# Moving a seven-product block form from six gate chunks to nine other projection chunks, on one Trainium2 core

## The chip, the cores and the metric

The kernel runs on one core of a Trainium2 chip. TensorE (PE) multiplies, VectorE (DVE), ScalarE (ACT) and GpSimd (POOL) do the rest, SyncE (SP) issues nearly all loads. The metric is the device time of one execution in microseconds, lower is better. All arithmetic that matters here is in float32; each float32 matmul stands in the trace as two records.

## The reference, cut to what matters

256 tokens of width 1024 pass through two layers:

```
# first block
proj = norm(x) @ w_in            # heads of three attention branches A, B, M, their z, and 3072 gate logits
o_a, o_b, o_m = attention(...)   # sparse, latent and memory attention, 512 wide each
branch_n = (o_n * silu(z_n)) @ w_branch[n]
x = x + sum_n(sigmoid(gates_n) * branch_n) @ w_out
# second block
x = x + mixer(norm(x))           # dq, dk, dv: differential attention; gq, gk, gv, gg, gr: gated linear attention; w_o
x = x + cross_attention(norm(x), norm(mem_2))   # keys and values: mem_2 @ w_ckv, 1024 x 2048
x = x + mixture_of_experts(norm(x))             # 32 experts of 3 matrices, 201 MB of weights in all
```

## The kernel before, in words

**Chunks and slots.** The projection weights come in chunks of mostly 1024 x 512 (2 MB), listed in `chunks` (lines 300 to 344) in the order of use: mk, mv, cq, small, qi, uq, ukv, qa, ka, va, za, zb, qm, zm, then gate00, gate01, wb0, gate10, gate11, wb1, gate20, gate21, wb2, then wout0, wout1, ckv0, gr, gqk, dq, dk, gv, ckv1, gg, dv, ckv2, wo0, wo1, ckv3, wcq0, wcq1, wco0, wco1. Chunk c goes to slot c % 4 of `ring`; SP waits, chunk by chunk in this order, until the job that read the chunk four before it has ended (line 1134). After them come the experts' weights, 96 loads of 2 MB into ten buffers (lines 1156 to 1190); those of the first round are held back by `wcq`, by attention C and by x3, later ones by the expert job that read the buffer before.

**Projections on TensorE.** `project` (line 488) keeps 128 tokens x 128 inputs of x stationary and streams 512 columns of weights: 16 matmuls for a chunk, the result by tokens. `project_t` (line 513) keeps weights stationary and streams the 256 tokens: 32 matmuls for a chunk, the result transposed. Both write one of two PSUM banks `ACC` of 1024 columns, taken in turn; a job waits until the bank's user two jobs before has been drained. `spread` and the `after` arguments put attention steps (`attend`: scores S, transposes T, outputs O) between the matmuls of a chunk. VectorE masks and normalizes the scores, ScalarE takes the exponentials and copies the transposes.

**The block form** (`project_blocks`, line 624) is used for the six gate chunks. Weights and x are each cut into 2 x 2 blocks; seven products of blocks replace eight, as in Strassen's scheme in Winograd's form. The weight block is stationary, in tiles of 128, and 128 tokens stream: 7 x 8 = 56 matmuls of 128 columns. A job takes two `ACC` banks, "low" for four products and "high" for three. The sums of blocks of x (`T_x`) and of weights (`S_a`, `S_b`, and two made in place) are POOL's (lines 1291 to 1318): of each gate chunk four additions of 1024 columns, each followed by a wait for itself; the first may start when the chunk before has had its fourth product, the last after this chunk's fourth. VectorE's `gate_blocks` (line 1931) combines the products in eight operations of 256 columns, which read PSUM; ScalarE then takes the tanh from SBUF.

**The order around it.** TensorE: zb with attention A; qm; zm with attention B; gate00 and gate01 with attention M; wb0; gate10, gate11, wb1; gate20, gate21, wb2; transposes of mem_2; wout0, wout1; ckv0, in which x1 is transposed; gr, gqk, gate_z; dq, dk, gv, ckv1; transposes of dq and dk; the GLA products ("intra", "kend"); gg; states; dv; ckv2 and ckv3 with attention DA; wo, wcq, attention C, wco, router, experts. VectorE's order (line 1923 on): heads of A, A, heads of qm, B, M, merging of the three branches (line 1967), `drain_rows` of mem_2, a reciprocal root (`rsqrt`, line 1658, 12 small steps each waiting for the one before), x updated from wout0 and wout1 (`add_to_x`), the norm of x1 (line 2002), the decay chain of the gated attention (lines 2009 to 2019, with eight scans), the padding products (line 2027, six operations, each of two SBUF inputs), heads of dq and dk (line 2030). ScalarE drains qm, dq, dk, gv and the ckv chunks from PSUM with copies. Between decay steps (`decay_a`, `decay_e`) ScalarE takes exponentials (lines 1547 to 1550); on `decay_e` POOL makes the three products QP, QN, KE (line 1333), which TensorE needs for "intra".

A line that sets the pace of the loads, and the two that take a bank:

```
1134  wait_full(sp, last_job[chunks[c - RING][0]])
472   if n >= 2:
473       pe.wait_ge(acc_free[n % 2], n // 2)
```

Of the kernel before, what the change touches and what calls it, by code (L numbers as in the profile page):

```python
# [20 lines left out]
ALU = mybir.AluOpType  # L21
# [3 lines left out]
P = 128  # L25
D = 1024
S = 256
# [18 lines left out]
RING = 4  # L46
# [10 lines left out]
def two_block_layer(nc, A, out):  # L57
    ctx = ExitStack()
    with ctx:
# [128 lines left out]
        gate_chunks = [f"gate{n}{h}" for n in range(3) for h in range(2)]  # L188
        T_x = R2[:, :].rearrange("p (i k q) -> p i k q", i=4, k=4)
        S_a, S_b = (R5[:, 2048 + 1024 * i:3072 + 1024 * i].rearrange("p (k n) -> p k n", k=4) for i in range(2))  # L190
# [44 lines left out]
        x_sums = sem("x_sums")  # L235
        w_sums = sem("w_sums")
        block_products = sem("block_products")
        gate_sums = sem("gate_sums")
        gate_tanh = sem("gate_tanh")
# [97 lines left out]
        ckv_chunk(2)  # L337
        for h in range(2):
            chunks.append((f"wo{h}", 512, [(0, cols(A["w_o_2"][0], h * 512, h * 512 + 512))]))
        ckv_chunk(3)  # L340
# [5 lines left out]
        landed_value, seen = [], [0] * RING  # L346
        for c, (_, _, parts) in enumerate(chunks):
            seen[c % RING] += 16 * len(parts)
            landed_value.append(seen[c % RING])

        def slot_of(name):
            c = chunk_at[name]
            width = chunks[c][1]
            k = SLOT // width
            return slots[c % RING][:, 0:k * width].rearrange("p (k n) -> p k n", k=k)
# [3 lines left out]
        acc_no, aux_no, aux_uses, last_job = {}, {}, [0] * 4, {}  # L359
# [70 lines left out]
        for t in range(TT):  # L430
# [20 lines left out]
        stream = [slots[4], slots[5]] + [slots[chunk_at[name] % RING] for name in ("wcq0", "wcq1")] + spare[0:2] + [  # L451
            slots[chunk_at[name] % RING] for name in ("wco0", "wco1")] + spare[2:4]
# [15 lines left out]
        def _(pe):  # L468
            def acc(key):
                n = len(acc_no)  # L470
# [150 lines left out]
            def x_block(i, j):  # L621
                return XT3[:, 4 * i:4 * i + 4, j * P:(j + 1) * P]

            def project_blocks(name, after=None):

                c = gate_chunks.index(name)
                wait_chunk(name)
                w = slot_of(name)

                def w_block(i, j):  # L630
                    return w[:, 4 * j:4 * j + 4, 256 * i:256 * i + 256]

                if c == 0:
                    pe.wait_ge(x_sums, 4)
                low, low_full = acc((name, "low"))
                products = [(w_block(0, 0), x_block(0, 0), None, False), (w_block(0, 1), x_block(1, 0), None, True),
                            (S_a, T_x[:, 0], 1, False), (S_b, T_x[:, 1], 3, True),
                            (w_block(1, 0), T_x[:, 2], 3, False), (w_block(1, 1), T_x[:, 3], None, True),
                            (S_b, x_block(1, 1), 4, False)]
                for m, (left, right, sums, last) in enumerate(products):  # L640
# [3 lines left out]
                    if sums:  # L644
                        pe.wait_ge(w_sums, 4 * c + sums)
                    for j in range(2):
                        for k in range(4):
                            mm = nc.tensor.matmul(bank[:, j * P:(j + 1) * P], left[:, k, j * P:(j + 1) * P], right[:, k, :],  # L648
                                                  start=(k == 0), stop=(k == 3))
                            if m == 6 and (j, k) == (1, 3):  # L650
                                mm.then_inc(high_full, 1)
                            elif last and (j, k) == (1, 3):
# [3 lines left out]
                            if after:  # L656
                                after(m * 8 + j * 4 + k + 1)
                last_job[name] = (name, "high")
# [95 lines left out]
            project("qm", XT3)  # L754
# [8 lines left out]
            def start_m(done):  # L763
# [5 lines left out]
                if done == 14:  # L769
# [4 lines left out]
                if done in (14, 22, 30, 38):  # L774
                    attend("M", (done - 14) // 8, (done - 14) // 8 + 1)

            def end_m(done):
                if done in (6, 18, 30):
                    attend("M", 4 + (done - 6) // 12, 5 + (done - 6) // 12)

            project_blocks("gate00", start_m)
            project_blocks("gate01", end_m)
# [3 lines left out]
            for n in (1, 2):  # L786
                project_blocks(f"gate{n}0")
                project_blocks(f"gate{n}1")
# [8 lines left out]
            def merged_half(i):  # L797
                if i % 4 == 0:
                    pe.wait_ge(merged_ready, i // 4 + 1)

            R1T = kt(R1[:, :], KD)
            project("wout0", R1T, ready=merged_half)
            project("wout1", R1T)

            wait_turned("mem2")
            project("ckv0", R2T, after=lambda done, total: turn_rows("x1", 1) if done == total - 3 else None)
# [9 lines left out]
            project("dq", XT3)  # L816
            project("dk", XT3)
            project("gv", XT3)
            project("ckv1", R2T)
# [21 lines left out]
            project("gg", XT3)  # L841
# [284 lines left out]
        def _(sp):  # L1126
# [5 lines left out]
            for c, (name, width, parts) in enumerate(chunks):  # L1132
                if c >= RING:
                    wait_full(sp, last_job[chunks[c - RING][0]])
                for first, src in parts:
# [5 lines left out]
                    sp.dma_start(dst, src).then_inc(slot_landed[c % RING], 16)  # L1141
# [5 lines left out]
                if name == "wout0":  # L1147
                    wait_full(sp, ("gate21", "high"))
# [62 lines left out]
        def _(pool):  # L1211
# [83 lines left out]
            for t in range(TT):  # L1295
                for h in range(2):
                    wait_full(pool, ("kb", t, h))
            xb = [[XT3[:, 4 * i:4 * i + 4, j * P:(j + 1) * P] for j in range(2)] for i in range(2)]
            add(T_x[:, 0], xb[0][1], xb[0][0], ALU.subtract, x_sums, 1)
            add(T_x[:, 1], xb[1][1], T_x[:, 0], ALU.subtract, x_sums, 2)  # L1300
            add(T_x[:, 2], xb[1][1], xb[0][1], ALU.subtract, x_sums, 3)
            add(T_x[:, 3], T_x[:, 1], xb[1][0], ALU.subtract, x_sums, 4)
            for k in range(2):
                wait_full(pool, ("S", first_unit["B"] + len(units["B"]) - 1 - k))
            for c, name in enumerate(gate_chunks):
                pool.wait_ge(slot_landed[chunk_at[name] % RING], landed_value[chunk_at[name]])
# [965 lines left out]
```

## Time and profile before

| | |
|---|---|
| median of 3 runs | 1144.57 us (1144.38 to 1144.93) |
| the profiled execution | 1144.48 us, span 1142.8 us |
| granted TensorE clock, mean | 0.925 |
| busy: TensorE, VectorE, ScalarE, POOL | 83%, 30%, 15%, 9% |
| HBM traffic | 290 MB |

A profile is read from the whole to the part: which stretch is bound by what (the table of stretches), what an instruction takes start to start in a dense stretch (the timeline of one engine), and which wait ended last. In rows of the timeline the first number is the start in us, the second the length of the group, in brackets the idle time before it and what ended it. BIG, R, PJ and SQE are names of buffers in SBUF, buffer numbers left out.

### The profile page before, as it was taken

What the parts mean: (1) busy time and instruction counts of PE and PEld (TensorE: products, weight loads), DVE (VectorE), ACT (ScalarE), POOL (GpSimd) and SP (SyncE); (2) the same over time, 40 slices, a digit from 0 to 9 for tenths busy, and PEclk for the clock granted to TensorE, in tenths of its full rate; (3) what the DMA queues carried; (4) which work ended last, traced back from release to release, by engine and by line L of the source; (5) the groups of instructions that cost most, each with busy time, mean ns of one, the idle gap of its engine ahead of it and who ended that gap; (6) DMA issues with size and microseconds to landing.
All of it is one profiled execution on the core that took longest, in us unless ns stands there. A gap on an engine that the chain in (4) does not pass through costs nothing.

```text
span 1142.8 us, 11530 instructions
## 1 busy us (share of the span) xinstructions
PE 944.0 (83%) x4742; PEld 532.3 (47%) x4742; DVE 341.3 (30%) x879; ACT 175.3 (15%) x380; POOL 102.6 (9%) x121
## 2 busy tenths in 40 slices
PE   7999999899999999999999999665655556474737
PEld 3555485679999465455544554221221213131312
DVE  3217934764232221525644523100010101010101
ACT  2114232441000012212311312000000000000000
POOL 2013110135343010100000000000000000000000
PEclk9999999999999999999999999888777869787879
DMA  9546232224444264432208548999999999999996
GB/s 328 175 157 218 83 142 74 74 74 145 151 148 180 81 220 147 147 125 96 74 1 316 205 191 356 428 428 428 427 428 428 427 428 428 427 427 428 428 421 271
DMA packets 64308, 290.33 MB, mean 254 GB/s; under 512 B 9015, under 2 KB 11902, under 8 KB 52222
## 3 DMA queue, kind: packets, MB, share of 16 engines
q1 hardware_dynamic: 63966, 289.04, 63.9%
q8 instruction: 39, 0.64, 0.2%
q10 hardware_dynamic: 288, 0.52, 0.1%
q14 instruction: 15, 0.12, 0.0%
HBM read 288.51 MB, written 1.05 MB: 253 GB/s over the span
## 4 chain that ended last, share of the span: by engine, by line
PE 63%; DMA 28%; DVE 5%; ACT 2%; issue 1%; SPq 0%; DVEq 0%; ACTq 0%
PE ACC L505 24%; PE ACC L520 8%; PE AUX L1038 6%; PE ACC L648 6%; DMA ring<-in_w_e_up_dram 5%; PE ACC L544 4%; PE AUX L1074 4%; DMA BIG<-in_w_e_up_dram 3%; DMA ring<-in_w_e_down_dram 3%; DMA PJ<-in_w_e_up_dram 3%; DMA PJ<-in_w_e_gate_dram 3%; DMA BIG<-in_w_e_down_dram 3%; DMA SQE<-in_w_e_down_dram 3%; DMA SQE<-in_w_e_gate_dram 3%; DMA ring<-in_w_e_gate_dram 3%; PE ACC L930 2%
## 5 line engine op out<-in xcount | busy, mean ns | idle before, releaser
L505 PE MATMUL ACC<-ring,BIG 128*128 128x512 f32 (+2 forms) x384 | 159.1, 574 | 0.2 <-ACT BIG L1531 0.2
L1038 PE MATMUL AUX<-ring,R 128*32 128x512 f32 x416 | 113.3, 708 | 54.0 <-DMA BIG<-in_w_e_up_dram 21.5
L505 PE MATMUL ACC<-ring,R 128*128 128x512 f32 (+1 forms) x296 | 129.2, 591 | 2.8 <-DVE R L1697 2.1
L505 PEld LDWEIGHTS ACC<-ring,BIG 128*128 128x128 f32 x384 | 72.5, 190 | 81.6 <-issue 73.6
L520 PE MATMUL ACC<-BIG,ring 128*128 128x256 f32 (+1 forms) x464 | 106.9, 384 | 0.0
L520 PEld LDWEIGHTS ACC<-BIG,ring 128*128 128x128 f32 (+1 forms) x464 | 84.8, 187 | 16.1 <-issue 4.1
L505 PEld LDWEIGHTS ACC<-ring,R 128*128 128x128 f32 x296 | 55.8, 192 | 65.5 <-issue 64.2
L1038 PE MATMUL AUX<-R 128*32 128x512 f32 x112 | 61.9, 717 | 25.2 <-DMA ring<-in_w_e_gate_dram 14.4
L1038 PE MATMUL AUX<-BIG,R 128*32 128x512 f32 x192 | 55.6, 745 | 28.1 <-DMA PJ<-in_w_e_up_dram 21.3
L2207 DVE SCALAR_TENSOR_TENSOR R<-R,AUX 128x512 f32<-128x512 f32 x8 | 5.5, 686 | 232.5 <-ACT R L1626 232.5
L1038 PEld LDWEIGHTS AUX<-ring,R 128*32 128x32 f32 x416 | 28.3, 129 | 92.9 <-issue 92.9
L1038 PE MATMUL AUX<-PJ,R 128*32 128x512 f32 x192 | 53.2, 717 | 19.2 <-DMA ring<-in_w_e_up_dram 11.6
L1074 PE MATMUL AUX<-ring,BIG 128*32 128x512 f32 x192 | 52.3, 705 | 11.8 <-DMA SQE<-in_w_e_down_dram 5.8
L1038 PE MATMUL AUX<-SQE,R 128*32 128x512 f32 x112 | 62.0, 718 | 0.0
L544 PE MATMUL ACC<-ring,BIG 128*128 128x512 f32 x128 | 55.8, 593 | 0.9 <-DMA ring<-in_w_cq_dram 0.9
L2209 DVE SCALAR_TENSOR_TENSOR R<-R,AUX 128x512 f32<-128x512 f32 x8 | 8.4, 1050 | 138.1 <-PE AUX L1038 138.1
L1074 PE MATMUL AUX<-PJ,BIG 128*32 128x512 f32 x128 | 34.5, 701 | 11.7 <-DMA ring<-in_w_e_down_dram 11.7
L1708 DVE TENSOR_REDUCE MS<-SQE 128x8 f32<-128x1024 f32 (+4 forms) x13 | 18.0, 1382 | 74.3 <-ACT SQE L1372 63.3
L1407 ACT ACTIVATE SQE<-SQE,SMALL 128x256 f32<-128x256 f32 (+1 forms) x64 | 29.4, 460 | 60.7 <-DVE SMALL L1746 60.7
L544 PEld LDWEIGHTS ACC<-ring,BIG 128*128 128x128 f32 x128 | 23.9, 190 | 29.3 <-issue 29.3
L1038 PEld LDWEIGHTS AUX<-R 128*32 128x32 f32 x112 | 14.0, 130 | 49.7 <-issue 49.7
L1038 PEld LDWEIGHTS AUX<-BIG,R 128*32 128x32 f32 x192 | 13.6, 134 | 48.9 <-issue 48.9
(313 smaller groups left out, 1290.1 us busy)
## 6 DMA issues: line engine op xcount, KB each, us to landing
ring<-in_w_in_dram SPq DMA_DIRECT2D x20, 2048.0 KB, 7.8
ring<-in_w_e_gate_dram SPq DMA_DIRECT2D x14, 2048.0 KB, 27.0
ring<-in_w_e_up_dram SPq DMA_DIRECT2D x12, 2048.0 KB, 29.8
ring<-in_w_e_down_dram SPq DMA_DIRECT2D x10, 2048.0 KB, 30.3
BIG<-in_w_e_up_dram SPq DMA_DIRECT2D x8, 2048.0 KB, 32.4
PJ<-in_w_e_gate_dram SPq DMA_DIRECT2D x6, 2048.0 KB, 27.6
BIG<-in_w_e_down_dram SPq DMA_DIRECT2D x6, 2048.0 KB, 27.5
PJ<-in_w_e_down_dram SPq DMA_DIRECT2D x6, 2048.0 KB, 34.6
```

The source lines that it names most:

```text
L505: mm = nc.tensor.matmul(bank[:, t * 512:t * 512 + width], lhs[:, i, t * P:(t + 1) * P], w[:, i, a:a + width], start=(i == 0), stop=(i == k ...
L520: mm = nc.tensor.matmul(bank[0:m, j * S:(j + 1) * S], w[:, i, a + j * P:a + j * P + m], rhs[:, i, :], start=(i == 0), stop=(i == k - 1))
L544: mm = nc.tensor.matmul(bank[:, c:c + 512], lhs[:, i, t * P:(t + 1) * P], w[:, i, :], start=(i == order[0]), stop=(i == order[-1]))
L648: mm = nc.tensor.matmul(bank[:, j * P:(j + 1) * P], left[:, k, j * P:(j + 1) * P], right[:, k, :], start=(k == 0), stop=(k == 3))
L930: mm = nc.tensor.matmul(ACC[t][:, h * 512:(h + 1) * 512], XT3[:, i, t * P:(t + 1) * P], slot_of(f"wco{h}")[:, i, :], start=False, stop=Fal ...
L1038: mm = nc.tensor.matmul(bank[r, :], M_xt[:, k, r], w[e][:, k, :], start=(k == 0), stop=(k == KD - 1))
L1074: mm = nc.tensor.matmul(AUX[2 + h][r, :], M_hidt[:, k, r], w[e][:, k, h * 512:(h + 1) * 512], start=(k == 0), stop=(k == 3))
L1407: last = a_.activation(e[:, i, :], e[:, i, :], ACT.Exp, bias=stat(u, 0)[:, i:i + 1], accum_out=stat(u, 1)[:, i:i + 1])
L1708: v.tensor_reduce(MS[:, 0:groups], squares.rearrange("p (g w) -> p g w", g=groups), AX_X, ALU.add).then_inc(squares_used, 1)
L2207: link(v.scalar_tensor_tensor(out=M_gated, in0=M_gated, scalar=1.0, in1=AUX[2][:, :], op0=ALU.add, op1=ALU.mult))
L2209: v.scalar_tensor_tensor(out=permuted, in0=M_gated.rearrange("q (p k) -> q p k", k=4), scalar=0.5, in1=AUX[3][:, :].rearrange("q (p k) -> ...
```

## The change

- The six gate chunks go back to `project_t`; ScalarE takes their tanh directly from PSUM, VectorE's merging waits for that.
- Nine other chunks take a block form: qm, wout0, wout1, ckv0, dq, dk, gv, ckv1, gg. It is row-stationary: 128 tokens of a block of x (or of a sum) are stationary and 256 weight columns stream, 7 x 4 = 28 matmuls of 256 columns; the result is by tokens.
- POOL makes the weight sums of the nine, each sum in four operations of 256 columns (`add_steps`), and the x sums for qm; VectorE makes the x sums for wout0/wout1, for ckv0/ckv1 and for dq, dk, gv, gg (`row_sums`, four operations of 512 columns) and combines all nine chunks' products (`combine`, parts 0 to 3, some placed apart). ScalarE's copies of these chunks go; ckv0 and ckv1 are scaled in place in SBUF.
- The fourth ring slot holds the sums `S_a`, `S_b` and `T_x` up to gg. Chunks use three slots until then; wo1 and wco1 are the ones that use the fourth. ckv3 is loaded ahead of wo0 and wo1.
- Order: VectorE combines dq between its log-decay and the scans, dk after the scans, gv around the heads of dq and dk. POOL's queue is qm, pads, wout0, wout1, ckv0, pads, dq, dk, then QP, QN, KE, then gv, ckv1, gg. The clearing of ATT moves behind ckv1.

The diff, cut to its core:

```diff
-        gate_chunks = [f"gate{n}{h}" for n in range(3) for h in range(2)]
+        block_chunks = ["qm", "wout0", "wout1", "ckv0", "dq", "dk", "gv", "ckv1", "gg"]
+        WS = slots[RING - 1]
...
+        c = chunk_at["ckv2"]
+        slot_no = [i % (RING - 1) for i in range(c + 3)] + [RING - 1] + [i % (RING - 1) for i in range(c, c + 3)] + [RING - 1]
...
+                products = [(w11, x[0][0], 0, 0), (w12, x[1][0], 0, 0), (S_a, T[:, 0], 1, 1), (S_b, T[:, 1], 3, 2),
+                            (w21, T[:, 2], 0, 3), (w22, T[:, 3], 0, 4), (w12, x[1][1], 4, 0)]
...
+                                mm = nc.tensor.matmul(bank, right[:, k, :], left[:, k, :], start=(k == 0), stop=(k == 3))
...
-            project_blocks("gate00", start_m)
-            project_blocks("gate01", end_m)
+            m_part = spread("M", 0, 4, begin=12)
+            project_t("gate00", XT3, after=start_m)
+            project_t("gate01", XT3, after=spread("M", 4, 7))
...
+            def add_steps(out, a, b, op, counter, value):
+                for k in range(4):
+                    ins = g.tensor_tensor(out[:, k, :], a[:, k, :], b[:, k, :], op)
+                ins.then_inc(counter, 1)
+                pool.wait_ge(counter, value)
+            def weight_sums(name):
...
+                if c:
+                    pool.wait_ge(block_products, 3 * c - 1)
+                add_steps(S_a, w21, w22, ALU.add, w_sums, 4 * c + 1)
+                add_steps(w21, w11, w21, ALU.subtract, w_sums, 4 * c + 2)
+                add_steps(S_b, S_a, w11, ALU.subtract, w_sums, 4 * c + 3)
...
+                pool.wait_ge(block_products, 3 * c + 1)
+                add_steps(w12, w12, S_b, ALU.subtract, w_sums, 4 * c + 4)
...
             pool.wait_ge(decay_e, 1)
             g.tensor_tensor(QP, kt(GQ, 2), kt(EP, 2), ALU.mult)
             g.tensor_tensor(QN, kt(GQ, 2), kt(EN, 2), ALU.mult)
             g.tensor_tensor(KE, kt(GK, 2), kt(EE, 2), ALU.mult).then_inc(gla_products, 1)
+            for name in ("gv", "ckv1", "gg"):
+                weight_sums(name)
...
+            for h in range(2):
+                combine(f"wout{h}", by_rows(TMP))
+                part = X3[:, :, h * 512:(h + 1) * 512]
+                v.scalar_tensor_tensor(out=part, in0=TMP, scalar=0.25, in1=part, op0=ALU.mult, op1=ALU.add).then_inc(x_added, 1)
+                dve.wait_ge(x_added, h + 1)
+                if h == 0:
+                    dve.wait_ge(rows_squared, 4)
+                    rsqrt(2, SMALL[:, 64:66], SMALL[:, 78:80]).then_inc(mem2_scaled, 1)
+                    row_sums(T_mem2, quarters(R2T), mem2_sums)
```

In `combine`, part 0 copies one product and adds another, part 1 has two additions, part 2 three (after which the low bank is free), part 3 one (the high bank); each part waits for its products.

## Rows read from the trace of the kernel before

**Rows 1.** The table of stretches: window, length, busy time by engine, granted clock, DMA share, GB/s
```profile
760.00:1143.00 383.00, 234.49 (x1576) 86.73 (x1568) 33.46 (x69) 15.22 (x28) 0.00 (x0) 0.81 0.98 415
...
218.00:222.00 4.00, 4.00 (x17) 2.98 (x16) 1.88 (x4) 0.90 (x5) 0.00 (x0) 0.63 0.01 2
...
241.00:279.00 38.00, 36.36 (x294) 34.82 (x290) 21.57 (x38) 10.32 (x26) 15.26 (x7) 1.00 0.32 111
```

**Rows 2.** TensorE's timeline, chunks: wb0, gate10, wb1, ckv1, the transposes behind, end of wb2
```profile
278.74 14.02 PE L520 MATMUL ACC<-BIG,ring 128*128 128x256 f32 x64
292.60 3.73 PE L648 MATMUL ACC<-BIG,ring 128*128 128x128 f32 x32
...
317.65 12.72 PE L520 MATMUL ACC<-BIG,ring 128*128 128x256 f32 x58
...
475.38 13.90 PE L505 MATMUL ACC<-ring,R 128*128 128x512 f32 x32
489.11 1.91 PE L555 MATMUL AUX<-ident,PJ 128*128 128x128 f32 x16
...
370.41 1.91 PE L555 MATMUL AUX<-ident,BIG 128*128 128x128 f32 x16
```

**Rows 3.** TensorE's timeline: first scores of A, qm, a wait in B, gate00, DA's scores
```profile
160.46 0.61 PE L675 MATMUL AUX<-R 128*128 128x128 f32 x4
...
187.74 14.00 PE L505 MATMUL ACC<-ring,BIG 128*128 128x512 f32 x32
...
214.68 0.71 PE L675 MATMUL AUX<-R 96*128 96x128 f32 x4 [1.17 <-DVE SQE L1742]
...
241.13 0.71 PE L648 MATMUL ACC<-BIG,ring 128*128 128x128 f32 x4
...
531.20 0.61 PE L675 MATMUL AUX<-R 128*128 128x128 f32 x4
```

**Rows 4.** Timeline around qm's norm: ScalarE's drain, POOL's x sum, VectorE
```profile
201.78 1.09 ACT L1378 ACTIVATE PJ<-ACC 128x512 f32<-128x512 f32 x2 [13.49 <-PE ACC L505]
...
206.75 1.26 POOL L1292 TENSOR_TENSOR R<-BIG 128x512 f32<-128x512 f32 x1 [59.32 <-PE AUX L555]
206.85 1.19 DVE L1675 SCALAR_TENSOR_TENSOR NW<-NW 128x8 f32<-128x8 f32 x1
...
214.21 0.42 DVE L1742 SCALAR_TENSOR_TENSOR SQE<-AUX,causal 128x256 f32<-128x256 f32 x1
```

**Rows 5.** POOL: two operations of 256 columns, and the group of 1024 columns
```profile
142.47 0.74 POOL L1255 TENSOR_TENSOR BIG<-PJ 128x256 f32<-128x256 f32 x1 [24.98 <-DVE PJ L1723]
143.16 0.73 POOL L1256 TENSOR_TENSOR BIG<-PJ 128x256 f32<-128x256 f32 x1
...
L1292 POOL TENSOR_TENSOR R<-ring 128x1024 f32<-128x1024 f32 x6 | 14.5, 2411 | 20.9 <-PE AUX L675 20.5
```

**Rows 6.** Timeline of POOL and VectorE at the gated products and the padding
```profile
466.51 1.27 POOL L1333 TENSOR_TENSOR PJ<-BIG 128x512 f32<-128x512 f32 x1 [50.21 <-ACT BIG L1550]
466.67 1.66 DVE L2027 TENSOR_TENSOR BIG<-BIG 64x512 f32<-64x512 f32 x1
```

**Rows 7.** VectorE's timeline: a root's first step, the scaling behind it, the scans
```profile
403.53 0.17 DVE L1661 TENSOR_SCALAR NW<-SMALL 128x2 f32<-128x2 f32 x1 [2.41 <-ACT BIG L1362]
...
405.90 1.42 DVE L1684 TENSOR_SCALAR BIG<-BIG,RS 128x1024 f32<-128x1024 f32 x2
...
439.25 1.57 DVE L2014 TENSOR_TENSOR_SCAN SQE<-ones,SQE 128x64 f32<-128x64 f32 x8
```

**Rows 8.** ScalarE's timeline: start of the exponentials
```profile
462.95 1.28 ACT L1547 ACT_TABLE_LOAD   x1
```

**Rows 9.** Loads to landing (size, median us); a VectorE and a TensorE wait for a load
```profile
ring<-in_w_in_dram SPq DMA_DIRECT2D x20, 2048.0 KB, 7.8
...
41.69 1.22 DVE L1708 TENSOR_REDUCE MS<-SQE 128x8 f32<-128x1024 f32 x1 [10.89 <-DMA GF<-in_norm_ffn_dram]
...
610.92 7.11 PE L544 MATMUL ACC<-ring,BIG 128*128 128x512 f32 x16 [0.91 <-DMA ring<-in_w_cq_dram]
```

More of the change, by code:

```diff
@@ L795, in _ @@
                     turn(2 * t + g, ("mem2", t, g))
-            def merged_half(i):
-                if i % 4 == 0:
-                    pe.wait_ge(merged_ready, i // 4 + 1)
             R1T = kt(R1[:, :], KD)
-            project("wout0", R1T, ready=merged_half)
-            project("wout1", R1T)
+            pe.wait_ge(merged_ready, 1)
+            project_blocks("wout0", R1T, T_x, merged_sums, after=lambda done: pe.wait_ge(merged_ready, 2) if done == 4 else None)
+            project_blocks("wout1", R1T, T_x, merged_sums)
             wait_turned("mem2")
-            project("ckv0", R2T, after=lambda done, total: turn_rows("x1", 1) if done == total - 3 else None)
+            project_blocks("ckv0", R2T, T_mem2, mem2_sums, after=lambda done: turn_rows("x1", 1) if done == 20 else None)
             wait_turned("x1")
@@ L1322, in _ @@
             g.memset(QPAD, 0.0).then_inc(pads_cleared, 1)
-            g.memset(ATT, 0.0)
             link(g.memset(causal[:, 128:256], 0.0))
             g.memset(causal[0:64, 192:256], NEG).then_inc(pads_cleared, 1)
+            for name in ("wout0", "wout1", "ckv0"):
+                weight_sums(name)
             wait_full(pool, ("x1", 1, 1))
@@ L1516, in _ @@
             act.wait_ge(mem2_scaled, 1)
-            square_rows(3, X3, ZTv, ["wout0", "wout1"])
+            square_rows(3, X3, ZTv, [(x_added, 2)])
             def drain_mem2(key, T3, c):
@@ L1525, in drain_mem2, with scale_mem2 @@
                 last.then_inc(free_sem(key), 1)
-            drain_mem2("ckv0", R1v, 0)
+            def scale_mem2(key, T3, c):
+                wait_drained(act, key)
+                for t in range(TT):
+                    part = T3[:, t, c:c + 512]
+                    last = a_.activation(part, part, ACT.Copy, scale=SMALL[:, 78 + t:79 + t])
+                link(last)
+            scale_mem2("ckv0", R1v, 0)
             drain("gr", [(GRT[:, :], lambda b: b[0:16, 0:S])])
@@ L1987, in _ @@
                             link(ins)
[L1989 to L2000 removed]
+            row_sums(T_x, quarters(kt(R1[:, :], KD)), merged_sums)
+            drain_rows("mem2", R2T, GC_MEM2)
+            TMP = R4[:, 0:1024].rearrange("p (t n) -> p t n", t=TT)
+            for h in range(2):
+                combine(f"wout{h}", by_rows(TMP))
[6 more added lines that the diff above has]
+                    row_sums(T_mem2, quarters(R2T), mem2_sums)
             norm_rows(3, X3, ZTv, 5)
+            combine("ckv0", by_rows(R1v, 0), range(2))
             drain_rows("x1", XT3, GC_MIX)
+            combine("ckv0", by_rows(R1v, 0), range(2, 4))
+            row_sums(T_x, quarters(XT3), x1_sums)
             lam = GB[:, GB_LAM:GB_LAM + 256].rearrange("p (a b d) -> p a b d", a=2, b=2)
```

289 lines of the change are left out of this document (147 added, 142 removed).

## The prediction

> **What bounds the kernel now.** I read the table of stages first. From 760 us to the end the DMA engines are 98% busy and TensorE only 234.5 of 383 us [rows 1]: the experts' weights set that pace, and their first loads wait for TensorE's earlier work. So up to about 699 us TensorE's chain decides, and what it gains or loses there shifts the end one for one. Then I read TensorE's timeline, start to start. A plain gate chunk takes 292.60 - 278.74 = 13.86 us; a gate chunk in the present block form (317.65 - 292.60) / 2 = 12.52; a projection of 16 matmuls of 512 columns 489.11 - 475.38 = 13.73 [rows 2]. The whole stretch is dense, with small waits such as the 1.17 for VectorE at 214.68 [rows 3]. Third, VectorE and POOL side by side, because the new form gives both much more to do.
>
> **The two forms.** A plain matmul of 256 columns is 13.86 / 32 = 0.433 us. The new form has 7 products of 4 such matmuls: 28 x 0.433 = 12.13 us, so 1.60 less than a projection. Nine chunks: -14.4. Giving the block form up costs 13.86 - 12.52 = 1.34 for each gate chunk.
>
> **Up to the gates.** POOL's sums of x now run from about 147.5 to 153 and qm's weight sums to about 162, when attention A has just begun; qm starts at 187.74 [rows 3]. qm then ends 1.7 earlier. ScalarE no longer drains it (two copies, 1.09 [rows 4]), which leaves VectorE's norm of the heads 2.4 earlier. POOL's x sums used to lie in that norm: a tiny two-input operation took 1.19 us beside POOL's 1.26 us operation at 206.75 [rows 4], and the norm ended only at 214.21. I work it out to 208.0, before the first scores of attention B instead of behind them. Attention A, which had no such wait, took 187.74 - 160.46 = 27.3 from its first scores. B, starting its scores at 207.7 with two more matmuls behind, should end at 235.6 instead of 241.13 [rows 3]: **-5.5** with qm.
>
> **The gates.** The first two with attention M take 278.74 - 241.13 = 37.6 now [rows 2, 3]; less 25.0 for the chunks that is 12.6, of which 38.00 - 36.36 = 1.6 is idle time [rows 1], behind a VectorE that POOL slows. In the plain form, with POOL silent there: 2 x 13.86 + 12.6 - 1.6 = 38.7, **+1.0**. The other four: 4 x 1.34 = **+5.4**. ScalarE reads their banks straight from PSUM; each bank is wanted again 6.9 us later at the earliest, against 1.09 for a read of one [rows 4], so that costs nothing.
>
> **Eight chunks from wout0 to gg** are dense today. They give 8 x 1.60 = **-12.8** if nothing waits. But POOL must now make four sums of 1024 columns for each within 12.13 us. A sum in quarters is four operations of 256 columns; such operations start 143.16 - 142.47 = 0.69 apart [rows 5], so a sum is about 2.85 with its semaphore, four 11.4. (A whole sum is 2.41 [rows 5]; a quarter of one, 0.60, is the lower bound for a quarter.) POOL is then busy nearly without a break, and the question is what VectorE loses beside it. At 466.51 POOL's and VectorE's operations start together: VectorE's first one takes 1.66 of which 1.11 pass until POOL's ends [rows 6]. So each VectorE operation with two SBUF inputs waits for the POOL operation in progress, a tiny one as well [rows 4]. Beside quarters, a step of 0.2 becomes about 0.8. Sums that read PSUM I leave at their price, as no row shows them slowed.
>
> The Trainium skill, "SBUF — State Buffer", section "Who interferes with whom", says that a VectorE instruction with two SBUF inputs and a POOL instruction that reads SBUF exclude each other for a whole instruction; by it the scans below wait too, as the sum has them. The rows agree where they show the pair; no row has a scan beside POOL.
>
> Stalls that follow (TensorE's time, from the end of wb2):
> - *ckv0.* After wout0 VectorE updates x, makes a reciprocal root of 12 steps (405.90 - 403.53 = 2.37 alone [rows 7]), four sums over the memory rows, then wout1's parts, the third of which frees the bank that ckv0 needs. Uncontended this ends in time. Beside POOL: the update until +15.8, the root 3 x 0.2 + 9 x 0.8 until +23.3, four sums of 0.65 with a quarter before each until +28.7, three parts until +31.6. TensorE wants the bank at +26.0: **5.7**. The same root for x1 and the parts ahead of gr cost **1.1** more. Lower end: if the root's steps don't wait, 0.4.
> - *gv.* dq starts (D) as now, with 0.3 more of a wait. VectorE's decay chain now stands behind dq's combination, which ends at D + 12.8. Its eight scans (1.57 alone [rows 7]) with a quarter before each end at D + 19.2, the two differences at D + 21.2. ScalarE's exponentials take 466.51 - 462.95 = 3.56 [rows 6, 8]: D + 24.8. Only then POOL may make its three gated products, ahead of gv's weight sums in its queue, alternating with VectorE's six padding operations: first sum at D + 35.3, wanted at D + 27.7, **7.6**; third sum at D + 41.3, wanted at D + 37.1, **4.2**. Lower end: with free scans and quarters of 0.60, 5.1 together.
> - *ckv1, gg.* POOL does not catch up (11.4 of 12.13 us), and VectorE's eight scalings and gains hold it 0.65 each; gv's bank is also freed late behind them. **4.4** and **1.8**. Lower end 2.4 together.
> Sum of stalls 5.7 + 1.1 + 0.3 + 7.6 + 4.2 + 4.4 + 1.8 = **+25.1**; lower end about 8.7.
>
> **Edits at no price.** With one slot less for loads, each is issued when the chunk three before it is done, so at least 15 us ahead, against 7.8 to land [rows 9]; without that cover it would cost those 7.8. The small vectors wait for mk's end now and land some 4 us later than 41.69 [rows 9]; VectorE, idle for them today, has nothing else to do until the latents are squared, after the chunk small. The x sums that VectorE makes for wout0 and dq are early enough. After attention DA, wcq1's load waits for ckv3 instead of the output projection: the wait at 610.92 goes, **-0.9** [rows 9]. The tanh of gg has 10 us of cover.
>
> **Sum.** -5.5 + 1.0 + 5.4 - 12.8 + 25.1 - 0.9 = +12.3. The profiled execution took 1144.48 (span 1142.8), and the median of the runs is 1144.57: no difference that matters. So 1144.5 + 12.3 = **1156.8 us**.
>
> **Rivals.**
> - *Small steps don't wait (0.2).* Roots and scans run at their own price and only the order of POOL's queue stalls TensorE. Then ckv0 loses 3.5, gv 7.0, ckv1 and gg 5.6, with 0.8 elsewhere, 16.9 in all: +4.1, **1148.6**. Against it: the 1.19 us step.
> - *POOL stays ahead: faster (0.15).* The place is POOL's chain of three sums before each chunk's fourth product. If quarters cost 0.60 and VectorE does not hold them, stalls are 8.7: -4.1, **1140.4**. It decides from stalls below 10.5: without stalls the balance is -12.8, and 2.3 of it is needed. For it: POOL's chain of 8.5 us fits in the 10.4 us between the earlier chunk's fourth product and this one's. Against it: gv's sums stand behind the exponentials whatever a quarter costs.
> - *The clock falls as well (0.15).* After the waits at 214 to 218 us the granted clock was 0.63 from 218 to 222 [rows 1], that is at the lower level for most of the stretch, which lost 1.5 us. Three long waits (ckv0, gv, ckv1) would add 4.5: **1161.3**. Where TensorE then waits for POOL anyway the slower clock costs nothing, so it is not in the sum. The Trainium skill, "TensorE: Matmul & The Clock Gate", section "What's actually happening", has the clock at half after idling; the row agrees.
> - *The new form isn't 12.13 (within the forecast's range).* Its stationary operand is x and a weight load goes with every 256 columns, as in the plain gate chunk, whose 13.86 already contains that.
>
> **How the numbers follow.** The forecast has 0.50, with its own range 1151 to 1161 (quarters of 0.64 instead of 0.69 take 3.6 off, a share of the clock's fall adds). The range of 8 in 10 reaches down through the second case to 1144 and up past the third to 1163; what lies below 1144 is the faster case. About 0.2% (2.3 us) is what a measurement of this kernel can tell from no change. Slower: 0.50 + 0.15 + most of the 0.2 = 0.79; faster 0.13; same 0.08, from the edges of the two lower cases.
>
> **What would show it.** Right: matmuls of the new form 0.433 apart; attention B without the wait at its first scores; POOL near nine tenths from wout0 to gg; TensorE waiting for VectorE at ckv0's start and for POOL at gv's third and fourth product; roots of 6 us or more beside POOL. Wrong: gv without a wait over 4 us, roots of 2.4 us beside POOL's quarters, or the stretch from the end of wb2 to attention DA's first scores (531.20 - 370.41 = 160.8 now [rows 2, 3]) shorter than before; forecast 173.

## The result, and the profile after

The changed kernel takes **1146.97 us** (median, 1145.34 to 1148.82) against 1144.92 of the kernel before on the same chips: ratio **1.0017, interval 1.0009 to 1.0024**. It is slower by about 2 us: the interval excludes no difference at all, but the difference is smaller than the 0.2% that the prediction took as what a measurement of this kernel can tell. The profiled execution took 1145.34 us (span 1143.5), 0.86 above the profiled one of before; it is the fastest of its 16, so the stretches below add up to less than the 2.05 between the medians. Forecast were 1156.8 us and "slower".

The stretches, before and after, between the same points of TensorE's chain:

| stretch | before | after | measured | forecast |
|---|---|---|---|---|
| start of gate00 | 241.13 | 233.84 | -7.3 | -5.5 |
| first two gates with M, to wb0 | 37.61 | 38.15 | +0.5 | +1.0 |
| wb0 to the end of wb2 | 91.67 | 96.69 | +5.0 | +5.4 |
| to attention DA's first scores | 160.79 | 164.90 | **+4.1** | **+12.3** |
| from there to the first experts' products | 168.24 | 167.11 | -1.1 | -0.9 |
| sum | | | +1.2 | +12.3 |

The table of stretches after (window, length, busy time by engine, granted clock, DMA share, GB/s):

```profile
218.00:222.00 4.00, 4.00 (x26) 3.20 (x23) 2.89 (x8) 1.41 (x7) 0.00 (x0) 1.00 0.00 0
368.68:533.58 164.90, 152.24 (x701) 122.81 (x700) 101.74 (x193) 24.72 (x38) 99.99 (x122) 0.97 0.37 128
398.00:402.00 4.00, 3.75 (x11) 3.14 (x12) 1.89 (x3) 1.98 (x3) 3.19 (x4) 0.61 0.99 379
466.00:470.00 4.00, 1.16 (x3) 0.98 (x4) 3.83 (x6) 0.00 (x0) 3.91 (x6) 0.50 0.02 4
470.00:474.00 4.00, 4.00 (x14) 3.27 (x13) 3.69 (x11) 0.00 (x0) 2.87 (x5) 0.65 0.00 0
760.00:1143.00 383.00, 236.26 (x1580) 86.89 (x1572) 33.51 (x69) 15.23 (x28) 0.00 (x0) 0.81 0.98 417
```

Against [rows 1]: the clock no longer falls at 218 us, but it falls twice between 398 and 474, and the last stretch is DMA-bound as before. In the second row VectorE is busy for 102 us and POOL for 100; before they had 50 and 8 (in 160.8 us). TensorE's timeline after:

```profile
207.41 0.61 PE L686 MATMUL AUX<-R 96*128 96x128 f32 x4
...
233.84 1.13 PE L531 MATMUL ACC<-BIG,ring 128*128 128x256 f32 x4
...
368.68 1.91 PE L566 MATMUL AUX<-ident,BIG 128*128 128x128 f32 x16
...
392.88 1.89 PE L657 MATMUL ACC<-ring,R 128*128 128x256 f32 x8
398.25 10.28 PE L657 MATMUL ACC<-ring,R 128*128 128x256 f32 x40 [3.49 <-DVE R L1969]
408.36 1.91 PE L566 MATMUL AUX<-ident,BIG 128*128 128x128 f32 x16
...
455.08 5.34 PE L657 MATMUL ACC<-ring,BIG 128*128 128x256 f32 x24
461.90 1.99 PE L657 MATMUL ACC<-ring 128*128 128x256 f32 x8 [1.47 <-POOL ring L1307]
468.84 7.38 PE L657 MATMUL ACC<-ring 128*128 128x256 f32 x24 [4.94 <-POOL ring L1307]
476.05 1.89 PE L657 MATMUL ACC<-ring,BIG 128*128 128x256 f32 x8
...
484.35 7.17 PE L657 MATMUL ACC<-ring,R 128*128 128x256 f32 x32 [1.23 <-POOL ring L1307]
...
498.82 3.69 PE L657 MATMUL ACC<-ring,BIG 128*128 128x256 f32 x16 [1.20 <-DVE R L2082]
...
533.58 0.61 PE L686 MATMUL AUX<-R 128*128 128x128 f32 x4
```

One product is four matmuls, and each matmul has two records, so x8 is one product, 1.73 us. The gaps in brackets are not all that is lost. From 398.25 twenty matmuls should take 20 x 0.432 = 8.65 us and end at 406.9; the next row is at 408.36, so 1.45 went to the low clock of 398 to 402. From 468.84 three products should end at 474.0; the next starts at 476.05, another 2.0 [the rows of 466 to 474 above]. All losses, start to start: ckv0 3.5 + 1.45; gv's third product 1.6, its fourth 5.2, then 2.0; ckv1 1.4; gg 1.4 and 0.5 in small ones. That is **17** (the small ones are what is left over), against 8 x (13.73 - 12.1) = 13.0 gained: +4.1.

VectorE and POOL after, the root of the memory rows, the row sums, the scans, the padding, and POOL beside them:

```profile
384.44 0.58 DVE L1680 TENSOR_SCALAR NW<-SMALL 128x2 f32<-128x2 f32 x1
...
387.09 0.16 DVE L1692 SCALAR_TENSOR_TENSOR NW<-NW 128x2 f32<-128x2 f32 x1
387.29 0.58 DVE L1694 SCALAR_TENSOR_TENSOR NW<-NW 128x2 f32<-128x2 f32 x1
...
391.33 0.68 DVE L1979 TENSOR_TENSOR R<-R 128x512 f32<-128x512 f32 x1
...
395.32 0.41 DVE L1961 COPY R<-ACC 128x256 f32<-128x256 f32 x1
...
445.38 4.06 DVE L2043 TENSOR_TENSOR_SCAN SQE<-ones,SQE 128x64 f32<-128x64 f32 x8
...
457.82 6.84 DVE L2057 TENSOR_TENSOR BIG<-BIG 64x512 f32<-64x512 f32 x6
...
497.19 0.72 DVE L2081 COPY_PREDICATED R<-past,ACC 128x512 f32<-128x512 uint32 x1 [5.20 <-POOL R L1324]
```

```profile
377.67 23.52 POOL L1307 TENSOR_TENSOR ring<-ring 128x256 f32<-128x256 f32 x28 [0.69 <-PE ACC L657]
...
454.03 1.27 POOL L1344 TENSOR_TENSOR PJ<-BIG 128x512 f32<-128x512 f32 x1 [1.78 <-ACT BIG L1565]
...
457.71 13.96 POOL L1307 TENSOR_TENSOR ring<-ring 128x256 f32<-128x256 f32 x16
```

ScalarE, the load of its table and the first of the four exponentials:

```profile
436.51 1.28 ACT L1562 ACT_TABLE_LOAD   x1
451.70 0.63 ACT L1562 ACTIVATE BIG<-BIG 128x512 f32<-128x512 f32 x1 [13.90 <-DVE BIG L2048]
```

The root takes 6.9 us (384.44 to 391.33) where a root alone takes 2.37 [rows 7]: ten of its twelve steps take about 0.6, two 0.16. The row sums take 4.0, the scans 0.51 each. POOL's 16 quarters from 457.71 take 0.87 each. The 1.4 at gg is not a wait for gg's own sums: VectorE's masks (497.19), which free the bank that gg takes, wait 5.2 us for the clearing of ATT (L1324), and that clearing now stands in POOL's queue behind three of gg's sums.

### The profile page after: what moved, and what is told of

The parts are those of the page before. It is cut to its first block, busy times and chain, and to the rows that moved or that the text cites. A ratio compares the mean times of both kernels' runs of the same rounds, so it can differ in the third digit from the quotient of the medians.

```text
span 1143.5 us, 11541 instructions
## 1 busy us (share of the span) xinstructions
PE 940.3 (82%) x4670; PEld 572.0 (50%) x4670; DVE 366.8 (32%) x915; ACT 171.1 (15%) x372; POOL 155.1 (14%) x241
## 4 chain that ended last, share of the span: by engine, by line
PE 60%; DMA 27%; DVE 5%; POOL 3%; ACT 2%; SPq 2%; issue 1%; POOLq 0%; DVEq 0%; ACTq 0%
PE ACC L531 15%; PE ACC L516 13%; PE AUX L1042 7%; PE ACC L657 7%; DMA ring<-in_w_e_gate_dram 5%; DMA ring<-in_w_e_down_dram 5%; PE ACC L555 5%; POOL ring L1307 3%; DMA SQE<-in_w_e_up_dram 3%; DMA BIG<-in_w_e_up_dram 3%; DMA PJ<-in_w_e_up_dram 3%; DMA PJ<-in_w_e_down_dram 3%; DMA BIG<-in_w_e_gate_dram 2%; PE AUX L1078 2%; PE ACC L934 2%; DMA SQE<-in_w_e_gate_dram 2%
## 5 line engine op out<-in xcount | busy, mean ns | idle before, releaser
L531 PE MATMUL ACC<-BIG,ring 128*128 128x256 f32 (+1 forms) x848 | 190.2, 381 | 0.0
L531 PEld LDWEIGHTS ACC<-BIG,ring 128*128 128x128 f32 (+1 forms) x848 | 157.6, 188 | 25.7 <-issue 3.8
L1307 POOL TENSOR_TENSOR ring<-ring 128x256 f32<-128x256 f32 x144 | 111.3, 804 | 147.2 <-DMA ring<-in_w_out_dram 74.6
L516 PE MATMUL ACC<-ring,BIG 128*128 128x512 f32 (+2 forms) x224 | 89.8, 559 | 0.0
L1042 PE MATMUL AUX<-BIG,R 128*32 128x512 f32 x192 | 54.9, 736 | 29.3 <-DMA PJ<-in_w_e_up_dram 21.0
L516 PE MATMUL ACC<-ring,R 128*128 128x512 f32 (+1 forms) x168 | 73.7, 589 | 2.8 <-DVE R L1716 2.1
L516 PEld LDWEIGHTS ACC<-ring,BIG 128*128 128x128 f32 x224 | 42.3, 190 | 44.0 <-issue 36.0
L657 PE MATMUL ACC<-ring 128*128 128x256 f32 x224 | 51.8, 390 | 6.4 <-POOL ring L1307 6.4
L657 PEld LDWEIGHTS ACC<-ring 128*128 128x128 f32 x224 | 43.8, 196 | 13.5 <-POOL ring L1307 7.2
L516 PEld LDWEIGHTS ACC<-ring,R 128*128 128x128 f32 x168 | 31.6, 194 | 35.8 <-issue 34.5
L1078 PE MATMUL AUX<-PJ,BIG 128*32 128x512 f32 x128 | 34.9, 707 | 12.1 <-DMA ring<-in_w_e_down_dram 12.1
L657 PE MATMUL ACC<-ring,R 128*128 128x256 f32 x160 | 37.3, 391 | 4.7 <-DVE R L1969 3.5
## 6 DMA issues: line engine op xcount, KB each, us to landing
ring<-in_w_e_down_dram SPq DMA_DIRECT2D x10, 2048.0 KB, 29.4
PJ<-in_w_e_gate_dram SPq DMA_DIRECT2D x6, 2048.0 KB, 27.3
```

Source lines behind the costliest of these rows:

```text
L516: mm = nc.tensor.matmul(bank[:, t * 512:t * 512 + width], lhs[:, i, t * P:(t + 1) * P], w[:, i, a:a + width], start=(i == 0), stop=(i == k ...
L531: mm = nc.tensor.matmul(bank[0:m, j * S:(j + 1) * S], w[:, i, a + j * P:a + j * P + m], rhs[:, i, :], start=(i == 0), stop=(i == k - 1))
L657: mm = nc.tensor.matmul(bank, right[:, k, :], left[:, k, :], start=(k == 0), stop=(k == 3))
L1042: mm = nc.tensor.matmul(bank[r, :], M_xt[:, k, r], w[e][:, k, :], start=(k == 0), stop=(k == KD - 1))
L1078: mm = nc.tensor.matmul(AUX[2 + h][r, :], M_hidt[:, k, r], w[e][:, k, h * 512:(h + 1) * 512], start=(k == 0), stop=(k == 3))
L1307: ins = g.tensor_tensor(out[:, k, :], a[:, k, :], b[:, k, :], op)
```

## The experiments

All but E1 are compared with the 1146.97 of the changed kernel. They ran on two chips, on which the kernel before had medians of 1144.54 (E1, E3, E4, E5) and 1145.37 (E2, E6, E8, E9) against the 1144.92 above, so each difference from the changed kernel is uncertain by some 0.5 us from that alone.

**E1: the gates alone.** The kernel before with its six gate chunks plain and nothing else changed.

```diff
-            project_blocks("gate00", start_m)
-            project_blocks("gate01", end_m)
+            project_t("gate00", XT3, after=start_m)
+            project_t("gate01", XT3, after=spread("M", 4, 7))
...
-                project_blocks(f"gate{n}0")
-                project_blocks(f"gate{n}1")
+                project_t(f"gate{n}0", XT3)
+                project_t(f"gate{n}1", XT3)
```

> The kernel before with only its six gate chunks in the plain form: POOL makes no sums at all, and no other chunk is in blocks. Measured so far, before against after: attention B ends 7.3 us earlier (241.13 to 233.84), the first two gates with M take 0.5 more, the other four with their wb chunks 5.0 more. Theory A: most of the 7.3 comes from POOL's four sums of x, which no longer lie beside the norm of qm. Then it shows here too: first scores of B at 210 to 211, B's end at 236.5 to 237.5, and the time is 0.5 to 1.5 us above that of the kernel before. Rival: the 7.3 comes from qm's shorter form and its missing copies. Then B ends at 240 to 241 here and the time is 4.5 to 5.5 above that of the kernel before.

Measured: 1145.99 us against 1144.54 of the kernel before, +1.4 (ratio 1.001, 1.0001 to 1.0019). TensorE's timeline, B's first scores and gate00:

```profile
210.48 0.61 PE L675 MATMUL AUX<-R 96*128 96x128 f32 x4
...
236.91 1.13 PE L520 MATMUL ACC<-BIG,ring 128*128 128x256 f32 x4
```

gate00 starts 4.2 us earlier than before, though attention A began 0.6 later in this execution: 4.8 of the 7.1 that the full change gains, counted from A's first scores, is POOL's work gone. By B's scores at 222.97 us before, 219.24 here, 4.3 of it is there: that is the x sums beside qm's norm, with the low clock that followed. The last 0.5 comes where POOL's weight sums for gate00 ran beside the end of B (before, VectorE's normalisation at 236.31 took 2.02 us, here 0.69). The other 2.3 lies ahead of B's first scores: qm's form is 1.6 shorter, and TensorE's wait there for ScalarE's copies falls from 1.0 to 0.3. The rival falls.

**E5: without POOL's sums.** Left out: POOL's work on the weight sums (2 columns each instead of 1024), and the products of S_a and S_b read a block of the weights.

```diff
-                for k in range(4):
-                    ins = g.tensor_tensor(out[:, k, :], a[:, k, :], b[:, k, :], op)
-                ins.then_inc(counter, 1)
+                g.tensor_tensor(out[:, 0, 0:2], a[:, 0, 0:2], b[:, 0, 0:2], op).then_inc(counter, 1)
...
-(S_a, T[:, 0], 1, 1), (S_b, T[:, 1], 3, 2)
+(w22, T[:, 0], 1, 1), (w11, T[:, 1], 3, 2)
```

> The changed kernel with POOL's weight sums cut to one operation of 2 columns each, and the products of S_a and S_b read a block of the weights instead: POOL's work on the sums is left out, all else stays. Theory A (everything lost from wout0 to gg is POOL's sums: VectorE held by them, their place in the queue, and the clock after the long waits): roots of 2.4 us, the stretch from the end of wb2 to attention DA's first scores 148 to 149 us instead of 164.9, TensorE waiting nowhere over 0.5 us, the time 15 to 17 below the changed kernel, about 1130.5. Rival 1: VectorE's own additional combinations and row sums hold the banks: ckv0 still waits over 1.5 us, the stretch is 152 or more. Rival 2: the experts' loads don't follow the whole of it: stretch 148 but the time falls by under 12.

Measured: 1133.47 us, 13.5 below the changed kernel. The stretch of [rows 2, 3] is 151.8 us instead of 164.9. TensorE's timeline and the table of stretches:

```profile
463.04 1.89 PE L657 MATMUL ACC<-ring,BIG 128*128 128x256 f32 x8
466.90 14.01 PE L657 MATMUL ACC<-ring,R 128*128 128x256 f32 x56 [1.97 <-DVE PJ L1967]
```

```profile
466.00:470.00 4.00, 3.10 (x9) 2.60 (x10) 3.93 (x8) 0.00 (x0) 0.00 (x0) 0.72 0.98 324
```

So 13.1 of the 17 us hang on POOL's sums, and the time follows 1:1 (rival 2 falls). The other 4 don't, and I had expected none: ckv1 waits 2.1 for gv's bank behind VectorE's own root and norm, and its 28 matmuls take 13.9 (the next row starts at 480.75) instead of 12.1, at a granted clock of 0.72 from 466 to 470. At gv VectorE is late even without POOL; rival 1 is right there and wrong at ckv0.

**E3: one root in place of two.**

```diff
-                    dve.wait_ge(rows_squared, 4)
-                    rsqrt(2, SMALL[:, 64:66], SMALL[:, 78:80]).then_inc(mem2_scaled, 1)
...
-            norm_rows(3, X3, ZTv, 5)
+            dve.wait_ge(rows_squared, 5)
+            link(rsqrt(4, SMALL[:, 64:68], SMALL[:, 76:80]))
+            for t in range(TT):
+                v.tensor_scalar(ZTv[:, t, :], X3[:, t, :], SMALL[:, 76 + t:77 + t], None, ALU.mult).then_inc(rows_normed, 1)
```

> The changed kernel, with the reciprocal root of the memory rows (2 columns, 12 steps between wout0's and wout1's combination) and that of x1 made as one root of 4 columns at x1's place. Theory A (the small steps' waits for POOL's quarters cause ckv0's wait): ckv0 starts at 395 without its wait of 3.5, and the clock's fall after it (1.45 us) goes too; but x1's own root then decides, with 20 products of ckv0 done at 403.5 and x1 normalised at 405 to 407, so 2 to 3 us come back as a wait for x1. In all 2 to 3 us less than the changed kernel, about 1144.5. Rival 1: the four row sums hold the combination, not the root: ckv0 waits 2.5 or more and the time falls by under 1. Rival 2: ckv0's wait was never worth anything, since x1 comes no sooner: the wait for x1 takes all of it, within 0.5 of the changed kernel.

Measured: 1144.25 us, -2.7 as theory A has it. TensorE's timeline (x1's transposes, 408.36 in the changed kernel) and a stretch:

```profile
401.12 3.72 PE L657 MATMUL ACC<-ring,R 128*128 128x256 f32 x16 [0.37 <-POOL ring L1307]
405.77 1.97 PE L566 MATMUL AUX<-ident,BIG 128*128 128x128 f32 x16 [0.93 <-DVE BIG L2027]
```

```profile
398.00:402.00 4.00, 3.63 (x17) 2.89 (x16) 1.91 (x5) 1.85 (x4) 3.84 (x7) 1.00 1.05 403
```

The wait for VectorE at ckv0's start and the low clock behind it are gone. Of their 5 us 2.4 come back before x1's transposes: 1.2 as the wait for x1, the rest at POOL's sums, for which TensorE now waits 0.6 us at wout1 and 0.4 at ckv0. The whole stretch takes 163.0 us, 1.9 less.

**E4: gv's sums first.**

```diff
+            weight_sums("gv")
             pool.wait_ge(decay_e, 1)
             g.tensor_tensor(QP, kt(GQ, 2), kt(EP, 2), ALU.mult)
...
-            for name in ("gv", "ckv1", "gg"):
+            for name in ("ckv1", "gg"):
```

> The changed kernel, with POOL's three gated products behind gv's weight sums instead of ahead of them. Theory A (POOL's in-order queue causes gv's stall): gv's third and fourth product start without their waits (1.6 and 5.2 us), its clock stays up (2.0 us), and part of it returns at ckv1's third product, which waits 2 to 4 us for the sums that now stand behind the three products. In all 4 to 6 less than the changed kernel, 1141 to 1143. Rival (VectorE's six padding operations hold POOL whatever the order): gv's fourth product still waits over 3 us and the time falls by under 1.5.

Measured: 1149.27 us, 2.3 **slower** than the changed kernel. Neither theory had that. TensorE's and VectorE's timelines:

```profile
464.57 5.45 PE L657 MATMUL ACC<-ring 128*128 128x256 f32 x24 [0.61 <-POOL ring L1307]
469.85 1.89 PE L657 MATMUL ACC<-ring,BIG 128*128 128x256 f32 x8
482.00 14.18 PE L657 MATMUL ACC<-ring,R 128*128 128x256 f32 x56 [10.26 <-DVE PJ L1970]
```

```profile
467.02 2.28 DVE L1728 TENSOR_REDUCE MS<-SQE 128x32 f32<-128x2048 f32 x1
...
470.80 1.19 DVE L1683 TENSOR_SCALAR NW<-NWI 128x32 int32<-128x32 int32 x1
...
477.82 0.42 DVE L1965 TENSOR_TENSOR PJ<-ACC,PJ 128x256 f32<-128x256 f32 x1
...
481.44 0.42 DVE L1970 TENSOR_TENSOR PJ<-ACC,PJ 128x256 f32<-128x256 f32 x1
```

gv's products now run with 0.6 of waiting, so the queue's order did cause gv's stall. But gv's second combination stands behind a sum over the heads and a root that POOL, never idle now, stretches to 8.5 us, so gv's bank comes free at 481.9, 10 us after its last product. In the changed kernel the same VectorE chain was nearly as late (bank free at 477.5, and only 0.4 us of it spent waiting for TensorE) and could not be seen: TensorE was being held at gv anyway.

**E2: whole sums.**

```diff
-                for k in range(4):
-                    ins = g.tensor_tensor(out[:, k, :], a[:, k, :], b[:, k, :], op)
-                ins.then_inc(counter, 1)
+                g.tensor_tensor(out, a, b, op).then_inc(counter, 1)
```

> The changed kernel with each of POOL's sums as one operation of 1024 columns instead of four of 256. Theory A (VectorE's step waits until the POOL operation in progress ends, whatever its length): POOL's chain is shorter by 4 x 0.4 us a chunk, but a root step beside it takes up to 2.4 us. The root of 12 steps, 6.9 us now with about 10 of them slowed, would be 18 to 24 us; ckv0 waits 12 us or more; the time is 15 to 30 above the changed kernel. Rival 1 (the two engines share the memory by the access, not by the instruction): the root stays at 6 to 8 us and the time within 2 of the changed kernel. Rival 2 (POOL's shorter chain decides at gv, where it was late): below the changed kernel.

Measured: 1154.59 us, +7.6: quarters are right, but I had expected at least 15. TensorE waits 7.2 us at ckv0 (expected: 12 or more), 3.5 for gv's sums and 8.4 for gv's bank. VectorE beside POOL, in the root:

```profile
390.47 0.16 DVE L1692 SCALAR_TENSOR_TENSOR NW<-NW 128x2 f32<-128x2 f32 x1
390.66 2.26 DVE L1689 TENSOR_TENSOR NW<-NW 128x2 f32<-128x2 f32 x1
...
393.16 2.20 DVE L1692 SCALAR_TENSOR_TENSOR SMALL<-NW 128x2 f32<-128x2 f32 x1
```

```profile
387.09 2.35 POOL L1306 TENSOR_TENSOR ring<-ring 128x1024 f32<-128x1024 f32 x1 [1.40 <-PE ACC L657]
390.56 7.59 POOL L1306 TENSOR_TENSOR ring<-ring 128x1024 f32<-128x1024 f32 x3 [1.13 <-PE ACC L657]
```

A step of 2 columns waits 2.2 us for one POOL operation to end, so the wait is for a whole instruction. But one step passes between two POOL operations and several while POOL waits (389.44 to 390.56), so three of the twelve steps are held and the root takes 8.5 us (386.80 to 395.28), not 20: its price is the number of POOL operations that it meets, not its steps times their length. The Trainium skill, "SBUF — State Buffer", section "Who interferes with whom", has the pair held for a whole instruction; the 2.26 agrees.

**E6: the last four gates in blocks again.**

```diff
-block_chunks = ["qm", "wout0", ...
+block_chunks = ["qm", "gate10", "gate11", "gate20", "gate21", "wout0", ...
...
-                project_t(f"gate{n}0", XT3)
-                project_t(f"gate{n}1", XT3)
+                for h in range(2):
+                    project_blocks(f"gate{n}{h}", XT3, T_x, x0_sums, turned=True)
```

> The changed kernel with the last four gate chunks in the block form of the kernel before (weights stationary, the same sums of x, POOL's sums in quarters), the first two plain. Theory A: the stretch of these chunks with their wb parts returns from 96.7 to 91.7 us, and as TensorE's chain is the bound, the time falls by 4.5 to 5.4, to 1141.6 to 1142.5. Rival (VectorE, held by quarters that follow each other without a break, now combines late): under 3.

Measured: 1141.46 us, -5.5. POOL makes these chunks' sums and VectorE combines them, as in the kernel before. TensorE's timeline, the start of wb0 and the end of wb2:

```profile
272.09 13.98 PE L532 MATMUL ACC<-BIG,ring 128*128 128x256 f32 x64
...
363.56 1.91 PE L567 MATMUL AUX<-ident,BIG 128*128 128x128 f32 x16
```

The stretch is 91.5 us again, without a wait of TensorE. POOL and VectorE have little else to do there, so the helpers of the block form cost nothing. The rival falls.

**E8: gv plain.**

```diff
-            project_blocks("gv", XT3, T_x, x1_sums)
+            project("gv", XT3)
...
+            drain("gv", by_token(GV, 0))
...
-            combine("gv", by_rows(GV), range(1))
```

> The changed kernel with gv alone as a plain projection, drained by ScalarE: POOL has four sums less and VectorE eight combinations less just where both are full. Between 450 and 480 us both engines were found full, so that moving POOL's products behind gv's sums only moved the wait to VectorE. Theory A: gv's loss of 8.8 us (1.6 and 5.2 of waits, 2.0 of clock) and the 1.4 at ckv1 go, the chunk costs 1.6 more: 7 to 9 less than the changed kernel, 1138 to 1140, and TensorE waits under 1 us from dk to the turn of dq. Rival (the pair of engines is short of time over the whole stretch, not at gv): the normalised dq and dk, or ckv1's sums, come late in its place and the time falls by under 5.

Measured: 1137.49 us, **-9.5**. TensorE's timeline, gv, ckv1 and the turn of dq:

```profile
456.71 1.89 PE L657 MATMUL ACC<-ring,BIG 128*128 128x256 f32 x8
458.44 13.90 PE L516 MATMUL ACC<-ring,BIG 128*128 128x512 f32 x32
472.17 12.25 PE L657 MATMUL ACC<-ring,R 128*128 128x256 f32 x56
484.26 1.91 PE L566 MATMUL AUX<-ident,PJ 128*128 128x128 f32 x16
```

No wait is left there: one chunk that TensorE does slower by 1.6 us makes the kernel 9.5 faster than the changed one, a little more than the 7 to 9 expected. The edit takes gv's sums from POOL and its combinations from VectorE at once, so it does not separate the two; E4 and E5 do. The rival falls.

**E9: E3, E6 and E8 together.**

> The changed kernel with three edits together: one root for the memory rows and x1, gv as a plain projection, the last four gate chunks in blocks. If the three add up (2.7 measured, about 8, about 5): 15 to 16.5 below the changed kernel, 1130.5 to 1132, which is below the kernel before by 13. Rival (they get in each other's way, or the experts' loads no longer follow): 1135 or more.

Measured: **1129.92 us**, ratio 0.9868 to the kernel before (0.9853 to 0.9883), 15.4 us faster than it and 17.1 faster than the changed kernel. The parts add up to 2.7 + 5.5 + 9.5 = 17.7; expected were 15 to 16.5. TensorE's timeline, the same two points as 368.68 and 533.58 above:

```profile
364.30 1.91 PE L567 MATMUL AUX<-ident,BIG 128*128 128x128 f32 x16
...
517.96 0.61 PE L687 MATMUL AUX<-R 128*128 128x128 f32 x4
```

153.7 us for the stretch, against 164.9 and 160.8.

## Why the prediction was wrong

**The bound was right.** What TensorE's chain gained before the experts, the time gained too: 13.1 us in its stretch and 13.5 in the time (E5), 5.2 and 5.5 (E6), 9.0 and 9.5 (E8, whose stretch goes from 370.02 to 525.93). I read the last stretch as bound by DMA whose start waits for that chain [rows 1], and it was.

**The gains were right, one too small.** A chunk of the new form takes 12.1 us (484.26 - 472.17 in E8). The gates cost 5.6 where 6.4 were forecast. B's first scores came at 207.4, forecast 207.7. But from there to gate00 it took 26.4 us where I took 27.9, attention A's 27.3 and two matmuls more. A's 27.3 contains 3.8 us of waits for ScalarE and VectorE; B's 26.4 contains 1.9. So a neighbour's time was taken with its waits. That is 1.5 of the 1.8 between -7.3 and -5.5; the other 0.3 is B's earlier start, 0.2 of it from qm's.

**The step that failed is the sum of the stalls, +25.1; it was 17.** 21.9 of mine were at ckv0, gv and ckv1, where 11.7 of waits were measured. The places were right, and at ckv0 and gv the causes too; the sizes were too large, but for gv's fourth product (4.2 forecast, 5.2 measured).
- *ckv0, 5.7 forecast, 3.5 measured.* Counted from the end of wb2 (368.68) the update ended at +15.7 as forecast (15.8), the root at +22.7 (23.3), the row sums at +26.6 (28.7), the parts at +29.4 (31.6). Most of the error is the row sums: I put a quarter before each of the four, 5.4 us; the first ran at its own 0.68, the others took 1.1 to 1.2, and they overlap by about 0.1 (4.0 in all). The root gave another 0.6 (6.9 for 7.5).
- *gv, 11.8 forecast, 6.8 measured.* From dq's start (432.56): the scans ended at +16.9, not 19.2, for they cost 0.51 each, not 0.8; ScalarE's exponentials took 2.3 us, not 3.56, because the 1.28 us load of the table that [rows 8] shows in front of them had been done long before, at 436.51, while ScalarE waited; POOL then made its three products (454.03 to 457.71) while VectorE was still in dk's combination, which reads PSUM, and met no padding operation. Each cause is a few us, and they follow one another: the third product started at +29.3, where I had its sum ready at 35.3 (a stall of 1.6 for 7.6). The rest of the padding and the heads' root ran beside the next two sums instead, which took 6.9 us for 6.0: the fourth product started at +36.3, not 41.3, but as the third had come so much sooner, its own stall was 5.2, not 4.2.
- *ckv1 and gg, 6.2 forecast, 2.8 measured.* While TensorE stood at gv, POOL caught up, and at ckv1 only the fourth product waited. The half of the 2.8 that is gg's comes from the moved clearing of ATT, which I had not priced. I had let the lateness of gv and that of ckv1 stand beside each other; a stall gives every other engine time.
- *x1's root, 1.1 forecast.* It met four quarters (4.4 us, from 402.31); no wait was seen, yet x1 was normalised at 408.1, only 0.2 before TensorE's transposes. E3 showed it as the next bound.

**The clock** was a rival (0.15) and is part of what is seen: 3.5 of the 17 us passed at the lower clock behind the waits of ckv0 and gv. I had argued that where TensorE waits anyway the slow clock costs nothing, and that was nearly so. At full clock TensorE would have come to x1's transposes at 406.9 and waited for x1 until 408.1. At gv, VectorE stood ready from 475.9 and waited 0.4 us for TensorE; its three combinations would have freed the bank at 477.1, where ckv1 started at 477.8. From these rows I estimate that the clock cost under 1 us of the total; what it hid were two VectorE chains just behind. The waits alone are 13.6 against 25.1, so the size was off by nearly a factor of two.

**The rivals.** "Small steps don't wait" is nearest by its number (1148.6) and wrong in its mechanism (steps of 0.6 beside quarters, 2.2 beside whole sums). "POOL stays ahead" needed stalls below 10.5 and they were 17. Of what I had said the profile would show, most is there: matmuls 0.433 apart, B without the wait, TensorE waiting for VectorE at ckv0 and for POOL at gv's third and fourth product, gv above 4. Not there are the 173 us of the stretch, which took 164.9; a POOL near nine tenths busy from wout0 to gg (0.96 from 374 to 401 us and 0.93 from 436 to 496, but 0.71 over the whole); and roots of 6 us or more, for only one of the three beside POOL's quarters took that (6.9; the heads' 5.1, x1's 4.4). The median lies in the range of 8 in 10 and below the forecast's own range.

**What E4 and E5 add to the working.** I put gv's stall down to POOL's queue alone. Two chains end there within a few us of each other, and I costed only the first to be seen: behind POOL's sums stands VectorE's norm, holding gv's bank. The prediction names that bank under ckv1 and gives it no price of its own. Removing the first alone made the kernel slower.

## What to carry to other kernels

When a change moves work onto two engines that exclude each other, add up both engines' operations between two deadlines, not each wait by itself: between dk and the turn of dq both were nearly full (from 454 to 478 us VectorE was busy for 20.6 of 24 us and POOL for 22.5, their waits for each other included), and the fix was less work there (one chunk plain, E8), not another order (E4). Use the cheaper form chunk by chunk, where its helpers are idle (E6), and return it where they are full. A forecast that adds stalls up must let each stall give the late engines time before the next is counted. The slow clock behind a long stall is to be added only where no other engine is nearly as late as TensorE.

## What was not expected of the hardware

- VectorE's steps with one SBUF input (TENSOR_SCALAR of 2 columns) wait as those with two do: 0.58 to 0.65 beside quarters, 1.19 beside POOL's products in E4, 0.17 alone.
- The waiting isn't a strict turn for turn: two of twelve steps passed at 0.16 beside POOL's unbroken quarters, and a chain of scans of 0.2 came to 0.51 each.
- Behind a wait of 2.0 us (E5, before ckv1) the granted clock was 0.72 over the window from 466 to 470, and ckv1 took 1.7 us longer. Behind waits of 1.2 us and less (ckv1 and gg in the changed kernel, x1 in E3) the products ran at their usual pace. The same wait of 4.9 us at gv's fourth product was followed by a loss of 2.0 us in the changed kernel, 2.9 in E3 and 2.8 in E6.
- The load of ScalarE's table at 436.51 ran ahead of the wait for VectorE, 15 us before the exponentials that need it. In the kernel before, it stood behind a drain that itself waited for TensorE, and so was part of the chain [rows 8]; the change took that drain away.
